# Decay matrices of a two-block transformer step: mask matmuls replaced by a rectified difference and a masked product

## Chip, cores and metric

The kernel runs on one core of one Trainium2 chip. The metric is the device time of one execution in microseconds (us), given as the median of several runs. Engines are named as in the profile: PE is TensorE's matmul, PEld its weight load, DVE is VectorE, ACT is ScalarE, POOL is GpSimd, SP is the engine that issues most DMAs.

## The reference

Two blocks work on x of 256 rows by 1024 columns in float32. The first has two layers of attention with a gated output product. The second has two hybrid layers; each runs attention and a state-space scan side by side, joins them in one output product and adds a gated feed-forward part. The scan works in two chunks of 128 rows, with 16 heads in 2 groups. Cut to what the change touches:

```
def segsum_exp(a):
    cs = jnp.cumsum(a, axis=-1)
    diff = cs[..., :, None] - cs[..., None, :]
    t = a.shape[-1]
    mask = jnp.tril(jnp.ones((t, t), dtype=bool))
    return jnp.exp(jnp.where(mask, diff, -jnp.inf))

a = jnp.transpose((dt * a_neg).reshape(bsz, nc, CHUNK, SSM_GROUPS, e), (0, 1, 3, 4, 2))
cb = jnp.einsum('bclgn,bcsgn->bcgls', cc, bc)
m_mat = cb[:, :, :, None] * segsum_exp(a)
y_diag = jnp.einsum('bcgels,bcsgep->bclgep', m_mat, xg)
```

`dt` is positive and `a_neg` negative, so `cs` never rises, so on the kept side of the triangle diff is at most 0. Every layer also starts with a root-mean-square norm of the rows.

## The kernel before

All large products run in two float32r parts: ACT rounds a weight tile (`hi`, line 1367), DVE subtracts (`lo`, line 1033), and PE multiplies three combinations (line 1178). Weights come in chunks of 1 MB in three rotating slots (`raw`); `hi` and `lo` of a chunk are made in two halves, two chunks ahead of their use. `build_schedule` writes one list of steps by hand. Every engine walks this list in order and carries out its part of each step, so an engine's queue is first in, first out, and the place of a step in the list sets what stands behind it on every engine.

A hybrid layer has eight **decay** steps, four heads each, which are written in four pairs: chunk 0 group 0, chunk 1 group 0, chunk 1 group 1, chunk 0 group 1. In one step

- PE puts the mask into a bank (line 1334: a bf16 matmul of `identb` with the mask spread over four heads) and adds the cumulative sum of each head (line 1340, four bf16 matmuls of 128 columns)
- ACT turns each head's 128 columns into `hyb_E` (line 1592, Exp with the other end's negative sum `hyb_ncs` as bias; the mask of -1e30 becomes 0)
- DVE multiplies by `hyb_cb`, the product B C (line 2015, `hyb_MT`)
- PE later multiplies `hyb_MT` with the values (step diag, line 1349, 8 program matmuls for a pair, 16 in the trace). A pair ends in a **join** on DVE (lines 2023 to 2031), a Square on ACT (line 1392), and for chunk 1 a product with the state (line 1355) before the join.

`hyb_cb` is copied from its bank on ACT in the step bback (line 1571). The four scratch banks of PSUM are handed out in turn, so a step that takes a bank waits until the step four banks earlier has freed it:

```
def bank(self):
    n = len(self.banks)
    b = Bank(n % NSCR, self.banks[n - NSCR] if n >= NSCR else None)
```

By this count the first diag of pair 1 takes the bank of the second decay step of that pair, which ACT frees (`b.freed = (s, "scalar")`), and the second decay step of pair 4 takes the bank that the join of pair 3 frees.

Three more places are touched. At the start of the program the second half of x is turned, rounded (`first_split`) and its weights, chunk 1, are rounded by the step second_weights. Between the blocks (step second_factor) four Squares of 128x512 (`square`) give the mean square for the first hybrid layer. At the end of the first hybrid layer DVE adds the residual (`added`, line 1865) and multiplies by the gain (`gained`, line 1802) before PE turns the result.

Of the kernel before, what the change touches and what calls it, by code (L numbers as in the profile page):

```python
# [66 lines left out]
C_SEL = C_MASK + 2 * QC + P  # L67
C_ALL = C_SEL + 32
M_SCAN, M_SEL = 2 * QC, 2 * QC + P


def constants():
# [26 lines left out]
    c[:, C_MASK + 2 * QC:C_SEL] = np.where(t > u, NEG, 0.0)  # L99
# [257 lines left out]
def norm_goes_on(sc, mid):  # L357


    def second_half():  # L360
        turn_x(sc, 1, 0)
        squares(sc, 0)

    def factors():
        turn_x(sc, 1, 1)
        squares(sc, 1)
        if mid:
            factor(sc, "first")
            normed_residual(sc)
        else:  # L370
            factor(sc, "h")

    def second_factor():
        squares(sc, 0)
        squares(sc, 1)
        factor(sc, "both")

    sc.soon += [second_half, factors] + [second_factor] * mid
# [169 lines left out]
def hybrid(sc, layer, w, last_gain):  # L548
# [27 lines left out]
    def bback():  # L576
        b1, b2 = sc.bank(), sc.bank()
        s = sc.step("bback", banks=(b1, b2), conv=scan["silu", 0])
        b1.freed = b2.freed = (s, "scalar")
# [46 lines left out]
    def do(f, *x):  # L626
        return [lambda: f(*x)]
# [39 lines left out]
    def next_gain():  # L667
# [3 lines left out]
        0: (do(decay, 1, 1, 0) + do(state, 1), do(decay, 1, 1, 1)),  # L671
        1: (do(turn_y, 0, 0) + do(scanned, 1, 1), do(turn_y, 0, 1) + do(decay, 1, 0, 0) + do(decay, 1, 0, 1)),
# [32 lines left out]
    if layer == 0:  # L705
# [7 lines left out]
        turn_x(sc, 0, 1)  # L713
        add(sc, b1, 1, 1)
        for m in range(M):
            times_gain(sc, 1, m)
# [30 lines left out]
def build_schedule(w):  # L747
# [30 lines left out]
def due(s):  # L778

    if s.kind == "second_weights":  # L780
        return [(1, 0), (1, 1)]
# [8 lines left out]
def half_of(c, half):  # L790
# [7 lines left out]
    "taps": ("tensor", "scalar"), "mid_gain": ("vector",), "square": ("scalar",), "meansq": ("vector", "gpsimd"), "newton": ("vector",), "added": ("vector",),  # L798
# [9 lines left out]
    "bback": ("tensor", "scalar"), "xback": ("tensor", "scalar", "gpsimd"), "state": ("tensor", "scalar"),  # L808
# [6 lines left out]
def build(nc, t):  # L815
# [41 lines left out]
    masks = keep("masks", [P, 2 * QC + P + 32], BF16)  # L857
    csum = keep("csum", [P, P], BF16)
    identb = keep("identb", [P, P], BF16)
# [38 lines left out]
    def plan(tag, hybrid_):  # L898
# [36 lines left out]
        if hybrid_:  # L935
# [19 lines left out]
            put("ncs", [P, M, SH])  # L955
            put("dif", [P, SH])
# [167 lines left out]
    def _(pe):  # L1124
# [10 lines left out]
        for s in sc.steps:  # L1135
# [194 lines left out]
            elif s.kind == "decay":  # L1330
# [3 lines left out]
                nc.tensor.matmul(bank[:, :], identb[:, :],  # L1334
                                 spread(masks[:, M_SCAN:M_SCAN + P].unsqueeze(1), [P, 4, P]), start=True, stop=False)
                for i in range(4):
# [3 lines left out]
                    last = nc.tensor.matmul(seg, spread(pick, [96, P]), csum[0:96, :], start=False, stop=i == 3)  # L1340
# [18 lines left out]
    def _(act):  # L1359
# [35 lines left out]
        for s in sc.steps:  # L1395
# [28 lines left out]
            elif s.kind == "square":  # L1424
# [4 lines left out]
                square_sum(h[:, s.m, s.n * 512:(s.n + 1) * 512], sumsq[:, 2 * s.m + s.n:2 * s.m + s.n + 1], s)  # L1429
            elif s.kind == "ev_kv":  # L1430
# [138 lines left out]
            elif s.kind == "bback":  # L1569
                act.wait_ge(sem["bback", "tensor"], s.i + 1)  # L1570
                nc.scalar.activation(Hb["cb"][:, :, :, :].rearrange("p m g l -> p (m g l)"),
                                     psum[4 + s.banks[0].at][:, :], ACT.Copy)
# [12 lines left out]
            elif s.kind == "decay":  # L1585
# [97 lines left out]
    def _(dve):  # L1683
# [46 lines left out]
        def set_up():  # L1730
# [4 lines left out]
            nc.vector.tensor_copy(identb[:, :], ident)  # L1735
# [40 lines left out]
        for s in sc.steps:  # L1776
# [51 lines left out]
            elif s.kind == "meansq":  # L1828
                sq, ms, _, _ = norm_parts(s)
                if s.what == "y":  # L1830
                    dve.wait_ge(sem["join", "scalar"], s.of)
                    done(ts(ms, sq, 1.0 / 512, EPS, ALU.mult, ALU.add), s)
                else:
# [144 lines left out]
            elif s.kind == "sums":  # L1978
                dve.wait_ge(sem["sums", "tensor"], s.i + 1)
                bank = psum[4 + s.bank.at]  # L1980
                chained(ts(Hb["ncs"][:, :, :].rearrange("p m s -> p (m s)"), bank[:, 0:32], -1.0, None, ALU.mult))
                tt(Hb["dif"][:, :], bank[:, 32:48], Hb["ncs"][:, 0, :], ALU.add)
# [97 lines left out]
```

## Time and profile before

| what | value |
|---|---|
| median of 3 runs | 880.14 us (880.09 to 880.61) |
| profiled execution, its own time | 879.62 us |
| its span, first to last instruction | 877.7 us |
| granted TensorE clock, mean | 0.998 |
| busy: PE, DVE, ACT, POOL | 864.6, 567.0, 512.4, 125.5 us |

The span is the time from the first to the last profiled instruction; the execution's own time is 1.9 us more. Busy time of PE is modelled at the ends of its matmuls. A row of the timeline gives start, duration, engine, line, operation, output<-inputs, shape and count, and in brackets how long the engine had been idle and what released it.

### The profile page before, as it was taken

The numbers are of one execution on the slowest core, as the hardware profiler recorded it, in microseconds if no ns is written. First come the engines' busy times: TensorE is split into PE (matmuls) and PEld (weight loads), VectorE is DVE, ScalarE is ACT, GpSimd is POOL, SyncE is SP. The second block draws the span as 40 slices with busy tenths as digits, with TensorE's granted clock in tenths as the row PEclk, the third lists the DMA queues.
The fourth block names the chain that finished last, engine by engine and source line by source line (L and its number), as shares of the span: only waits on it lengthen the run. The fifth ranks groups of instructions, "written<-read, shape, count | busy, mean of one in ns | idle before, by whom it ended". The sixth has DMA issues, their size and how long they took to land. (4 is left out here: it accounts for less than half of the span.)

```text
span 877.7 us, 12103 instructions
## 1 busy us (share of the span) xinstructions
PE 864.6 (99%) x4426; PEld 701.9 (80%) x4426; DVE 567.0 (65%) x1004; ACT 512.4 (58%) x911; POOL 125.5 (14%) x99
## 2 busy tenths in 40 slices
PE   8999999999999999999999999999999999999996
PEld 6877888778877878888888888877878888888885
DVE  6966866767766778755555446566887755555444
ACT  6668466765878865644444334768865644444332
POOL 0122054110153510000000000153410000000000
PEclk9999999999999999999999999999999999999999
DMA  8723563445444345655555555444245665555531
GB/s 308 277 65 119 171 200 134 145 144 173 149 139 144 99 143 186 210 183 187 192 192 190 194 191 171 147 142 144 97 144 168 212 196 192 190 178 178 194 124 48
DMA packets 94749, 146.15 MB, mean 167 GB/s; under 512 B 6500, under 2 KB 54884, under 8 KB 94692
## 3 DMA queue, kind: packets, MB, share of 16 engines
q1 hardware_dynamic: 92804, 139.52, 48.1%
q0 software_dynamic: 1296, 4.72, 1.7%
q10 hardware_dynamic: 592, 1.15, 0.4%
q8 instruction: 36, 0.59, 0.3%
q14 instruction: 21, 0.17, 0.1%
HBM read 144.32 MB, written 1.05 MB: 166 GB/s over the span
## 5 line engine op out<-in xcount | busy, mean ns | idle before, releaser
L1033 DVE TENSOR_TENSOR lo<-raw,hi 128x1024 fp32r<-128x1024 f32 (+1 forms) x244 | 300.5, 1258 | 117.3 <-ACT hi L1367 114.4
L1367 ACT ACTIVATE hi<-raw 128x1024 fp32r<-128x1024 f32 (+1 forms) x260 | 266.7, 1059 | 106.5 <-PE bank L1178 100.9
L1178 PE MATMUL bank<-hi,xT_hi 128*128 128x512 f32 (+2 forms) x736 | 290.4, 395 | 1.2 <-DVE lo L1033 0.5
L1178 PE MATMUL bank<-hi,xT_lo 128*128 128x512 f32 (+2 forms) x736 | 282.6, 384 | 0.0
L1178 PE MATMUL bank<-lo,xT_hi 128*128 128x512 f32 (+2 forms) x736 | 281.8, 383 | 0.0
L1178 PEld LDWEIGHTS bank<-hi,xT_hi 128*128 128x128 f32 x736 | 138.3, 188 | 32.3 <-issue 6.4
L1178 PEld LDWEIGHTS bank<-hi,xT_lo 128*128 128x128 f32 x736 | 138.2, 188 | 28.1
L1178 PEld LDWEIGHTS bank<-lo,xT_hi 128*128 128x128 f32 x736 | 138.5, 188 | 25.1 <-issue 0.5
L1178 PE MATMUL bank<-hi,hT 128*128 128x512 f32 x352 | 109.6, 390 | 0.0
L1178 PEld LDWEIGHTS bank<-hi,hT 128*128 128x128 f32 x352 | 66.1, 188 | 13.7
L1178 PE MATMUL bank<-lo,hT 128*128 128x512 f32 x176 | 68.5, 389 | 0.0
L1178 PE MATMUL bank<-hi,oT_hi 128*128 128x512 f32 x160 | 66.9, 418 | 0.0
L1178 PE MATMUL bank<-hi,oT_lo 128*128 128x512 f32 x160 | 62.6, 391 | 0.0
L1178 PE MATMUL bank<-lo,oT_hi 128*128 128x512 f32 x160 | 62.4, 390 | 0.0
L1466 ACT ACTIVATE silu_gate<-bank,rms 128x256 f32<-128x256 f32 x44 | 20.7, 475 | 53.5 <-PE bank L1178 53.5
L1033 POOL TENSOR_TENSOR lo<-raw,hi 128x1024 fp32r<-128x1024 f32 x16 | 39.0, 2445 | 68.4 <-ACT hi L1367 68.4
L1871 DVE SCALAR_TENSOR_TENSOR quarter<-bank,rms,silu_gate 128x256 f32<-128x256 f32 x44 | 19.3, 479 | 44.2 <-ACT silu_gate L1466 44.2
L2002 DVE SCALAR_TENSOR_TENSOR hyb_acc<-bank,taps,hyb_acc 128x255 f32<-128x255 f32 (+2 forms) x72 | 29.2, 475 | 25.1 <-ACT hyb_acc L1559 25.1
L1633 POOL TENSOR_TENSOR rms<-rms,power 128x2 f32<-128x2 f32 (+1 forms) x9 | 6.1, 675 | 251.3 <-DVE rms L1843 246.7
L1178 PEld LDWEIGHTS bank<-lo,hT 128*128 128x128 f32 x176 | 33.0, 188 | 6.7
L1413 ACT ACTIVATE hT<-bank 128x512 fp32r<-128x512 f32 x22 | 12.1, 596 | 42.1 <-PE bank L1126 42.1
L1178 PEld LDWEIGHTS bank<-hi,oT_hi 128*128 128x128 f32 x160 | 30.1, 188 | 7.1 <-issue 1.8
(247 smaller groups left out, 950.9 us busy)
## 6 DMA issues: line engine op xcount, KB each, us to landing
raw<-in_w_in SPq DMA_DIRECT2D x26, 1024.0 KB, 5.0
raw<-in_w_gate SPq DMA_DIRECT2D x44, 512.0 KB, 3.8
raw<-in_w_up SPq DMA_DIRECT2D x44, 512.0 KB, 4.8
raw<-in_w_down SPq DMA_DIRECT2D x22, 1024.0 KB, 4.8
raw<-in_w_out SPq DMA_DIRECT2D x20, 1024.0 KB, 5.0
raw<-in_w_in_b SPq DMA_DIRECT2D x10, 1024.0 KB, 5.0
raw<-in_w_in_a SPq DMA_DIRECT2D x8, 1024.0 KB, 7.1
raw<-in_w_in_a SPq DMA_DIRECT2D x4, 256.0 KB, 4.9
```

The costliest lines, as they stand in the source:

```text
L1033: return engine.tensor_tensor(lo[r][:, cols], raw[c.i % RAW][:, cols], hi[r][:, cols].bitcast(F32), ALU.subtract)
L1178: last = nc.tensor.matmul(bank[:, 0:wd], still[a], mv[r][:, off:off + wd], start=c.first and i == 0 and j == 0, stop=c.last and i == len(t ...
L1367: nc.scalar.activation(hi[c.i % SPLIT][:, cols], raw[c.i % RAW][:, cols], ACT.Copy)\
L1413: done(nc.scalar.activation(out, bank[:, :], ACT.Copy), s)
L1466: last = nc.scalar.activation(sil[s.i % 2][:, m, :], bank[:, 0:UPW], ACT.Silu, scale=rms[:, 1, m:m + 1])
L1633: nc.gpsimd.tensor_tensor(rs, ms, power[:, 0:1] if s.what == "out" else power[:, :], ALU.pow).then_inc(sem["meansq", "gpsimd"], 1)
L1871: last = stt(quarter[s.buf][:, m * UPW:(m + 1) * UPW], psum[2 * s.block["pair"] + m][:, UPW:2 * UPW], rms[:, 1, m:m + 1], sil[s.i % 2][:, ...
L2002: ins = stt(acc[:, tap:S], x[:, 0:S - tap], cw[:, 3 - tap, ct:ct + 1], acc[:, tap:S], ALU.mult, ALU.add)
```

## The change

It does seven things. The mask matmul of each decay step goes, and each head's matmul starts and stops its own columns. ACT computes Relu(cs - difference), four times 128 columns, then waits for the last of them and applies one Exp with scale -1 over all 512 columns in place; off the kept side of the triangle this gives numbers up to 1 instead of 0. The triangle is put into `hyb_cb` instead: its eviction moves from ACT to DVE and multiplies by `upper`, and the bank is freed by DVE. DVE makes a further copy `hyb_cs` in the step sums. In the output product the decay step 1,1,1 moves ahead of the state product and 1,0,0 moves from after turn_y(0,1) to before it. At the program's start the two halves of chunk 1 are rounded each ahead of one half of x. Between the blocks, two Squares over whole rows replace four over half rows and one DVE addition. At the end of the first hybrid layer the gain of row block 0 comes ahead of the addition of row block 1.

```
     def second_factor():
-        squares(sc, 0)
-        squares(sc, 1)
-        factor(sc, "both")
+        for m in range(M):
+            sc.step("row_square", m=m, added=sc.added[0, m])
+        a = sc.step("meansq", what="both", before=sc.steps[-1])
+        sc.rstd = sc.step("newton", what="both", before=a)
...
-        b1.freed = b2.freed = (s, "scalar")
+        b1.freed, b2.freed = (s, "vector"), (s, "scalar")
         scan["bback"] = s
...
     out_product(sc, w["out"], 12, {
-        0: (do(decay, 1, 1, 0) + do(state, 1), do(decay, 1, 1, 1)),
-        1: (do(turn_y, 0, 0) + do(scanned, 1, 1), do(turn_y, 0, 1) + do(decay, 1, 0, 0) + do(decay, 1, 0, 1)),
+        0: (do(decay, 1, 1, 0) + do(decay, 1, 1, 1) + do(state, 1), ()),
+        1: (do(turn_y, 0, 0) + do(scanned, 1, 1) + do(decay, 1, 0, 0), do(turn_y, 0, 1) + do(decay, 1, 0, 1)),
...
         turn_x(sc, 0, 1)
+        times_gain(sc, 1, 0)
         add(sc, b1, 1, 1)
-        for m in range(M):
-            times_gain(sc, 1, m)
+        times_gain(sc, 1, 1)
...
         first = [first_turn(sc, 1, m) for m in range(M)]
+        sc.step("second_weights")
         first_split(sc, first[0])
         sc.step("second_weights")
         first_split(sc, first[1])
...
     if s.kind == "second_weights":
-        return [(1, 0), (1, 1)]
+        return [(1, s.i)]
...
-                nc.tensor.matmul(bank[:, :], identb[:, :],
-                                 spread(masks[:, M_SCAN:M_SCAN + P].unsqueeze(1), [P, 4, P]), start=True, stop=False)
                 for i in range(4):
...
-                    last = nc.tensor.matmul(seg, spread(pick, [96, P]), csum[0:96, :], start=False, stop=i == 3)
+                    last = nc.tensor.matmul(seg, spread(pick, [96, P]), csum[0:96, :], start=True, stop=True)
...
+            elif s.kind == "row_square":
+                ended(act, s.added, "vector")
+                done(nc.scalar.activation(Hb["xs"][:, s.m, :], h[:, s.m, :], ACT.Square,
+                                          accum_out=sumsq[:, s.m:s.m + 1]), s)
...
-                nc.scalar.activation(Hb["cb"][:, :, :, :].rearrange("p m g l -> p (m g l)"),
-                                     psum[4 + s.banks[0].at][:, :], ACT.Copy)
...
-                                                ACT.Exp, bias=Hb["ncs"][:, m, hh:hh + 1])
-                done(last, s)
+                                                ACT.Relu, scale=-1.0, bias=Hb["cs"][:, m, hh:hh + 1])
+                link(act, "scalar", last)
+                e = Hb[f"E{s.i % 2}"][:, :, :]
+                done(nc.scalar.activation(e, e, ACT.Exp, scale=-1.0), s)
...
+                nc.vector.tensor_copy(Hb["cs"][:, :, :].rearrange("p m s -> p (m s)"), bank[:, 0:32])
...
+            elif s.kind == "bback":
+
+                dve.wait_ge(sem["bback", "tensor"], s.i + 1)
+                done(tt(Hb["cb"][:, :, :, :].rearrange("p m g l -> p (m g) l"),
+                        psum[4 + s.banks[0].at][:, :].rearrange("p (a l) -> p a l", l=P),
+                        spread(upper.unsqueeze(1), [P, 4, P]), ALU.mult), s)
```

ACT at pair 1 of a hybrid layer, before (`hyb_st` is the eviction of the state product; line numbers are those of each version):

```order
L1534 ACTIVATE oT_hi<-hyb_o 128x4x128 x2
L1367 ACTIVATE hi_65<-raw_62 128x1024
L1592 ACT_TABLE_LOAD
L1592 ACTIVATE hyb_E_133<-bank,hyb_ncs 128x128 x4
L1592 ACTIVATE hyb_E_134<-bank,hyb_ncs 128x128 x4
L1583 ACTIVATE hyb_st<-bank 128x512
```

The same place now:

```order
L1537 ACTIVATE oT_hi<-hyb_o 128x4x128 x2
L1366 ACTIVATE hi_65<-raw_62 128x1024
L1593 ACTIVATE hyb_E_132<-bank,hyb_cs 128x128 x4
L1597 ACT_TABLE_LOAD
L1597 ACTIVATE hyb_E_132<-hyb_E_132 128x512
L1593 ACTIVATE hyb_E_133<-bank,hyb_cs 128x128 x4
L1597 ACTIVATE hyb_E_133<-hyb_E_133 128x512
L1584 ACTIVATE hyb_st<-bank 128x512
```

Each group of four is followed by a wide Exp, and the table load stands behind the first group. There are as many table loads as before. ACT from pair 3 to pair 4, in the output product, before:

```order
L1592 ACT_TABLE_LOAD
L1592 ACTIVATE hyb_E_133<-bank,hyb_ncs 128x128 x4
L1583 ACTIVATE hyb_st<-bank 128x512
L1367 ACTIVATE hi_64<-raw_61 128x1024
L1592 ACTIVATE hyb_E_134<-bank,hyb_ncs 128x128 x4
L1367 ACTIVATE hi_65<-raw_62 128x1024
L1416 ACTIVATE oT_hi<-bank 128x4x128
L1392 ACTIVATE junk,rmy<-hyb_xs 128x512
L1367 ACTIVATE hi_65<-raw_62 128x1024
L1416 ACTIVATE oT_hi<-bank 128x4x128
L1592 ACTIVATE hyb_E_133<-bank,hyb_ncs 128x128 x4
L1592 ACTIVATE hyb_E_134<-bank,hyb_ncs 128x128 x4
```

The part of it from the Square of pair 3's join (`junk`) on, now:

```order
L1391 ACTIVATE junk,rmy<-hyb_xs 128x512
L1593 ACTIVATE hyb_E_132<-bank,hyb_cs 128x128 x4
L1597 ACTIVATE hyb_E_132<-hyb_E_132 128x512
L1366 ACTIVATE hi_65<-raw_62 128x1024
L1415 ACTIVATE oT_hi<-bank 128x4x128
L1593 ACTIVATE hyb_E_133<-bank,hyb_cs 128x128 x4
L1597 ACTIVATE hyb_E_133<-hyb_E_133 128x512
L1366 ACTIVATE hi_66<-raw_63 128x1024
```

The first step of pair 4 stands right behind the Square; the second stays behind a `hi` and an `oT_hi` and now also behind the first step's Exp. Both steps of pair 3 stand ahead of `hyb_st`. ACT at the program's start, where `hi_65<-raw_62` is chunk 1 and first_x_59 and first_x_60 are the second half of x, before:

```order
L1377 ACTIVATE hi_64<-raw_61 128x512 x3
L1422 ACTIVATE xT_hi<-first_x_58 128x4x128
L1422 ACTIVATE xT_hi<-first_x_59 128x4x128
L1367 ACTIVATE hi_65<-raw_62 128x1024 x2
L1422 ACTIVATE xT_hi<-first_x_60 128x4x128
```

Now:

```order
L1376 ACTIVATE hi_64<-raw_61 128x512 x3
L1421 ACTIVATE xT_hi<-first_x_58 128x4x128
L1366 ACTIVATE hi_65<-raw_62 128x1024
L1421 ACTIVATE xT_hi<-first_x_59 128x4x128
L1366 ACTIVATE hi_65<-raw_62 128x1024
L1421 ACTIVATE xT_hi<-first_x_60 128x4x128
```

The first half of chunk 1 now stands ahead of the first rounding of the second half of x; DVE's subtractions moved in the same way.

## Rows read from the trace of the kernel before

**Rows 1.** The page, busy time of each engine (us, share, instructions).

```profile
PE 864.6 (99%) x4426; PEld 701.9 (80%) x4426; DVE 567.0 (65%) x1004; ACT 512.4 (58%) x911; POOL 125.5 (14%) x99
```

**Rows 2.** Groups by line and form, PE: busy us, mean ns of one.

```profile
L1340 PE MATMUL bank<-csum,masks 96*128 96x128 bf16 x64 | 6.2, 218 | 0.0
L1334 PE MATMUL bank<-masks,identb 128*128 128x512 bf16 x16 | 6.2, 385 | 0.0
```

**Rows 3.** Chain that ended last, at a decay step: start, us on it.

```profile
624.97 0.23 PE bank L1334
625.20 0.22 PE bank L1340 x4
```

**Rows 4.** Timeline of ACT, DVE and PE at pair 1.

```profile
296.06 1.28 ACT L1592 ACT_TABLE_LOAD   x1
297.36 2.18 ACT L1592 ACTIVATE hyb_E<-bank,hyb_ncs 128x128 f32<-128x128 f32 x8
299.64 0.69 DVE L2015 TENSOR_TENSOR hyb_MT<-hyb_E,hyb_cb 128x512 f32<-128x512 f32 x1 [0.34 <-ACT hyb_E L1592]
299.90 1.90 PE L1349 MATMUL bank<-hyb_xg,hyb_MT 128*128 128x64 f32 x16
```

**Rows 5.** Timeline of ACT, DVE and PE at pair 2.

```profile
303.64 0.63 ACT L1392 ACTIVATE junk<-hyb_xs 128x512 bf16<-128x512 f32 x1 [1.70 <-DVE hyb_xs L2031]
305.22 2.16 ACT L1592 ACTIVATE hyb_E<-bank,hyb_ncs 128x128 f32<-128x128 f32 x8
307.47 1.11 DVE L2015 TENSOR_TENSOR hyb_MT<-hyb_E,hyb_cb 128x512 f32<-128x512 f32 x1 [0.34 <-ACT hyb_E L1592]
308.19 1.89 PE L1349 MATMUL bank<-hyb_xg,hyb_MT 128*128 128x64 f32 x16
```

**Rows 6.** Timeline of ACT, PE and DVE at pair 3 and its join.

```profile
316.92 1.14 ACT L1592 ACTIVATE hyb_E<-bank,hyb_ncs 128x128 f32<-128x128 f32 x4
321.41 2.22 PE L1349 MATMUL bank<-hyb_xg,hyb_MT 128*128 128x64 f32 x16
324.59 0.69 DVE L2023 TENSOR_TENSOR hyb_xs<-bank,hyb_xs 128x512 f32<-128x512 f32 x1 [0.38 <-PE bank L1355]
326.76 0.69 DVE L2031 TENSOR_TENSOR hyb_xs<-hyb_xs,hyb_z 128x512 f32<-128x512 f32 x1
```

**Rows 7.** Timeline of ACT and PE at pair 4.

```profile
327.49 0.63 ACT L1392 ACTIVATE junk<-hyb_xs 128x512 bf16<-128x512 f32 x1 [5.28 <-DVE hyb_xs L2031]
329.55 2.17 ACT L1592 ACTIVATE hyb_E<-bank,hyb_ncs 128x128 f32<-128x128 f32 x8
331.68 2.00 PE L1349 MATMUL bank<-hyb_xg,hyb_MT 128*128 128x64 f32 x16 [0.25 <-DVE hyb_MT L2015]
```

**Rows 8.** DMA issues at 4.0 to 4.8 us: KB, us from issue to landing.

```profile
raw<-in_w_in_a SPq DMA_DIRECT2D x1, 1024.0 KB, 8.6
```

**Rows 9.** Timeline at the start: SP (issues), ACT, DVE and PE.

```profile
4.49 20.95 SPq L1093 DMA_DIRECT2D raw<-in_w_in_a  x6
13.22 1.99 ACT L1367 ACTIVATE hi<-raw 128x1024 fp32r<-128x1024 f32 x2
14.30 2.36 DVE L1033 TENSOR_TENSOR lo<-raw,hi 128x1024 fp32r<-128x1024 f32 x2 [0.26 <-ACT hi L1367]
15.67 0.47 PE L1178 MATMUL bank<-hi,xT_hi 128*128 128x512 f32 x1 [0.55 <-DVE lo L1033]
```

**Rows 10.** Timeline of ACT and PE between the blocks.

```profile
223.42 0.63 ACT L1392 ACTIVATE junk<-h 128x512 bf16<-128x512 f32 x1 [0.47 <-DVE h L2043]
225.06 0.63 ACT L1392 ACTIVATE junk<-h 128x512 bf16<-128x512 f32 x1
228.80 0.47 PE L1178 MATMUL bank<-hi,xT_hi 128*128 128x512 f32 x1 [0.45 <-ACT hyb_q L1447]
```

**Rows 11.** Timeline of DVE and PE at the end of the first hybrid layer.

```profile
542.82 0.68 DVE L1865 TENSOR_TENSOR h<-bank,h 128x512 f32<-128x512 f32 x1
544.15 0.33 PE L1126 MATMUL bank<-cst,quarter 128*128 128x128 f32 x1 [0.20 <-DVE quarter L1802]
```

More of the change, by code:

```diff
@@ L66 @@
 C_MASK = C_KEEP
-C_SEL = C_MASK + 2 * QC + P
+C_SEL = C_MASK + 2 * QC
 C_ALL = C_SEL + 32
-M_SCAN, M_SEL = 2 * QC, 2 * QC + P
+M_SEL = 2 * QC
 def constants():
@@ L98, in constants @@
             c[:, at:at + P] = np.where(x, 0.0, NEG)
-    c[:, C_MASK + 2 * QC:C_SEL] = np.where(t > u, NEG, 0.0)
     for part in range(3):
@@ L797 @@
     "chunk": ("tensor", "scalar", "vector", "gpsimd"), "columns": ("tensor", "vector"), "first_turn": ("tensor", "vector"), "first_split": ("scalar", "vector"), "gained": ("vector",), "turn": ("tensor", "scalar", "vector"),
-    "taps": ("tensor", "scalar"), "mid_gain": ("vector",), "square": ("scalar",), "meansq": ("vector", "gpsimd"), "newton": ("vector",), "added": ("vector",),
+    "taps": ("tensor", "scalar"), "mid_gain": ("vector",), "square": ("scalar",), "row_square": ("scalar",), "meansq": ("vector", "gpsimd"), "newton": ("vector",), "added": ("vector",),
     "ev_kv": ("scalar",), "ev_q": ("scalar",), "ev_z": ("scalar",), "ev_x": ("scalar",),
@@ L807 @@
     "sums": ("tensor", "vector", "scalar"), "conv": ("tensor", "scalar", "vector"), "conv_silu": ("scalar",),
-    "bback": ("tensor", "scalar"), "xback": ("tensor", "scalar", "gpsimd"), "state": ("tensor", "scalar"),
+    "bback": ("tensor", "scalar", "vector"), "xback": ("tensor", "scalar", "gpsimd"), "state": ("tensor", "scalar"),
     "decay": ("tensor", "scalar", "vector"), "diag": ("tensor",), "off": ("tensor",),
@@ L856, in build @@
     cst = keep("cst", [P, C_KEEP])
-    masks = keep("masks", [P, 2 * QC + P + 32], BF16)
+    masks = keep("masks", [P, 2 * QC + 32], BF16)
     csum = keep("csum", [P, P], BF16)
-    identb = keep("identb", [P, P], BF16)
     ones = keep("ones", [P, P])
@@ L955, in plan @@
             put("ncs", [P, M, SH])
+            put("cs", [P, M, SH])
             put("dif", [P, SH])
@@ L1734, in set_up @@
             ts(sinks[:, 1, :], sinks[:, 0, :], -1.0, None, ALU.mult)
-            nc.vector.tensor_copy(identb[:, :], ident)
             chained(nc.vector.tensor_copy(masks[:, :], stage[:, :]))
@@ L1832, in _ @@
                     done(ts(ms, sq, 1.0 / 512, EPS, ALU.mult, ALU.add), s)
+                elif s.what == "both":
+                    ended(dve, s.before, "scalar")
+                    done(ts(ms, sumsq[:, 0:M], 1.0 / D, EPS, ALU.mult, ALU.add), s)
                 else:
@@ L2010, in _ @@
                 m, g = s.mg
-                ended(dve, s.bback, "scalar")
+                ended(dve, s.bback, "vector")
                 dve.wait_ge(sem["decay", "scalar"], s.i + 1)
```

## Prediction, made before the changed kernel ran

> **What bounds the kernel now.** I read the page's busy times first: PE is busy for 864.6 of 877.7 us, DVE for 567.0, ACT for 512.4 [rows 1]. So PE sets the time nearly everywhere, and an edit counts by what it takes off PE's queue and by what it makes PE wait for. ACT and DVE are idle a third of the time, but that is an average. So next I read, pair by pair, when ACT finishes `hyb_E`, when DVE has multiplied it, and when PE needs the product. In pair 1 the last Exp ends at 297.36 + 2.18 = 299.54, DVE's second product runs from 299.64 to 300.33, and PE starts its 16 passes at 299.90; the second eight need that product and start halfway, at about 300.8 [rows 4]. The cover is about 0.5 us. In pair 2 the second product ends at 307.47 + 1.11 = 308.58 and is needed at 308.19 + 0.9 = 309.1 [rows 5]: again 0.5 us. In pairs 3 and 4 there is none: the 16 passes take 2.22 instead of 1.90 [rows 4, 6], and PE waits 0.25 for the first product of pair 4 [rows 7]. So ACT and DVE are idle on average and just in time here. The second hybrid layer repeats the pattern; I work one layer and double it.
>
> **What is removed.** On the chain a mask matmul takes 0.23 and the four sums 0.22 [rows 3]. The 385 ns of the group rows is a modelled length of overlapping matmuls [rows 2], not a cost. Without the mask a step gives back 0.22; 16 steps give 16 x 0.22 = 3.5 us, or 0.44 a pair, if nothing else is late.
>
> The row shows four bf16 sums with four weight loads in 0.22, or 55 ns each [rows 3]. The Trainium skill (TensorE: Matmul & The Clock Gate, LDWEIGHTS) gives a load of 128 columns as columns/1.2 ns, 107 ns; by that, an estimate, four loads take 0.43 and a step without its mask would be no shorter. The row disagrees, although its first load could hide behind the mask; I keep that as a rival below.
>
> **What is added on ACT.** Four Exp of 128 columns are done after 1.14 [rows 6], and eight after 2.18, so a further group adds 1.04 [rows 4]. The trace has no Relu; its neighbour is this Exp: same bank, same width, one bias column. Bounds: a Square moves 512 columns in 0.63 in one instruction [rows 5], so four Relus that move as many can't take less than about 0.63; above, nothing points over 1.14. I take 1.14 and 1.04, since the neighbour has the same width and count, and width is what makes four narrow ones dear. The wide Exp of 512 columns from SBUF is nearest to that Square, 0.63; four narrow ones bound it from above, 1.14 [rows 6]. It waits for the last Relu, so nothing of it overlaps: a step ends 0.63 later than before and the second step of a pair 2 x 0.63 = 1.26 later. The next group may start about 0.1 before the Exp ends, as neighbours do, so I use 1.15 for a pair.
>
> Pair 1. Relu needs no new table, so the first group runs from 296.06 to 297.15 ahead of the load; load 1.28 and Exp 0.63 end at 299.05 [rows 4]. The second group ends at 300.05, its Exp at 300.7, its product at 301.4. The first diag takes the bank that this second step frees, so it can't start before 300.75, while PE without the masks would be there at 299.90 - 0.44 = 299.46. PE waits 1.3; set against before, everything behind is 300.75 - 299.90 = 0.85 late. Its second eight would start at 301.65, after the product.
>
> Pair 2. Its chain starts with PE's diag of pair 1 (join, Square, `hi`, then the steps), so it moves along with the 0.85. Within it, Exp of the second step ends 1.15 later, and the product at 308.58 + 1.15 = 309.75 against a need of 309.1 - 0.44 = 308.65: PE waits 1.1. Against before 0.65 is lost, if DVE's product still takes 1.11; if GpSimd no longer runs beside it and it takes 0.69 [rows 4, 5], 0.25. I take 0.35, so 1.2 since the layer's start.
>
> Pair 3. The second step now stands ahead of `hyb_st`: Relu from 315.6, load, Exp to 318.6, second step to 320.3, its product by about 321.4 (DVE's order has two `lo` ahead). That is in time for the second eight (321.41 - 0.44 + 0.9 = 321.9), so the excess of 0.32 [rows 4, 6] goes. PE would be 0.44 + 0.32 earlier, but the second step of pair 4 needs the bank of the join, which ends at 326.76 + 0.69 = 327.45 [rows 6]. The two `hi` behind `hyb_st` end about 1.4 later, and the `lo` and `oT_lo` ahead of the join with them; DVE is then free at about 324.75, 0.15 later than the join's start [rows 6]. So of 0.76 about 0.6 is kept as PE's lead and 0.2 or so is waited.
>
> Pair 4. Its first step no longer waits behind `hi` and `oT_hi`. Square at 327.65, first group from 328.3 to 329.4, Exp to 330.0. From Square to Exp there were 2.06 us before [rows 7], of which 0.6 was the Square; the remaining 1.45 of `hi` and `oT_hi` run now, to 331.4. Second group 1.14, Exp 0.63, product 0.69: 333.9. PE's second eight started at 331.68 + 0.9 = 332.6 [rows 7] and start now at 334.0. PE waits about 2.4 and everything behind is 1.4 late, counted from pair 3's start. This is the largest term: two steps that were issued back to back after `oT_hi` took 2.17 [rows 7], and now the second begins only there and is serial.
>
> Layer: 1.2 + 1.4 = 2.6 late, with the 8 masks (1.8) already taken off. Two layers: **+5.2**.
>
> **`hyb_cb` and `hyb_cs`.** DVE gains a masked product of 0.7 (as the bank-reading add, 0.69 [rows 6]) and a copy of 0.2 at points where it waits afterwards; ACT loses a copy. PE takes the bank more than 0.5 later. Cost nothing; up to 0.3 a layer if that cover is gone.
>
> **The start.** Chunk 1 is issued at 4.49 and lands 8.6 later, at 13.1 [rows 8, 9]. ACT already starts its `hi` at 13.22 [rows 9], so it can't come forward. What changes is that x's rounding (0.63) now waits behind it, and on DVE x's subtraction (0.69) comes after `lo` instead of before. `lo` still starts at about 14.3 and takes 1.2; x's part ends at 16.1, and PE starts at 16.15 instead of 15.67 [rows 9]. **+0.5**; at best 0, if the landing were earlier in most executions.
>
> **Between the blocks.** The second row's data is ready at 223.42; the last of four Squares starts at 225.06 and ends at 225.7 [rows 10]. Now the second whole-row Square starts at 223.42 and takes 1.05 (a `hi` of 1024 columns is half of 1.99 [rows 9]) and 0.2 for its sum: 1.1 earlier, and DVE saves an add of 0.2. PE's wait of 0.45 [rows 10] goes, and nothing else is that late: **-0.5**.
>
> **End of the first hybrid layer.** The add at 542.82 to 543.5 stands ahead of the gain for which PE waits 0.20 [rows 11]. Moved behind, it frees 0.6: **-0.3** at most with PE's restart; 0.2 by the row.
>
> **Sum.** 5.2 + 0.5 - 0.5 - 0.3 = +4.9 on the profiled 879.62 us (span 877.7 and 1.9 around it): 884.5. The median stands 0.5 above that execution, so the median comes to **885.0 us**.
>
> **Rivals.**
> - ScalarE keeps up, faster. At the lower bound of 0.63 a group, a pair takes 4 x 0.63 = 2.5 against 2.18, an extra of 0.3 that the cover of 0.5 hides. The products would be in time and only the savings were left: -3.5 for masks, -0.6 for the excess and the wait in pairs 3 and 4 (two layers, in part), -0.8 and +0.5 elsewhere: 880.1 - 4.4 = 875.7, say 876. For it: engines are a third idle. Against it: covers of 0.5 against 1.15. It decides where a pair's extra falls under 0.5. Chance 0.18.
> - Half covered, no change: pair 4's lateness is the one that I built from most pieces. Without it a layer loses 1.2 - 0.6 = 0.6, two 1.2, in all 881; with pair 2 free too, 880. Chance 0.12.
> - Later still: GpSimd slows both products of pair 2 (0.4 more a layer), the join of pair 3 slips by 0.3, and PE's waits run on into late `lo`: 2 x 0.7 to 2 x 1.5 more, 886.5 to 888. Chance 0.12.
> - The change doesn't shorten PE: the loads behind the removed masks are no longer hidden and fill the gap. PE waits for the products at every pair anyway, so most of these 3.5 us are spent in waits already and little comes on top: 885 to 888. Chance 0.04.
> - Forecast, 882.5 to 887.5: 0.54.
>
> **Numbers.** Differences under 0.2% (1.8 us) can't be told from no change. Slower: 0.54 + 0.12 + 0.04 = 0.70; same 0.12; faster 0.18. The range leaves out the faster case below 878 (0.15) and anything above 889: 878 to 889.
>
> **What would show it.** No row of line 1334; about 0.22 between groups of sums. PE waits for `hyb_MT` (line 2015 before) of 1 to 2.5 us: first diag of pair 1 about 0.85 late, the longest wait in pair 4's second half. ACT: Relu groups of 1.1, Exp of 0.63, the second pair-4 group starting after `oT_hi`. PE's first matmul of chunk 1 at about 16.1 and not at 15.67. No wait at 228.8 and 544. It is wrong if Relu or the wide Exp is much shorter than its neighbour, or if ACT reaches pair 4 earlier than its queue lets me see.

## Result, and the profile after

The changed kernel takes 888.58 us (median of 4 runs, 885.99 to 890.33) against 880.20 for the kernel before beside it (880.09 to 880.61). The ratio is 1.0094 with a 95% interval of 1.0082 to 1.0106: 8.4 us slower. The forecast was 885.0, in a range of 878 to 889, so direction and range held and the size came out 3.6 us short. But 888.58 lies above the forecast's own band (882.5 to 887.5) and above the times of all four rivals (888 at most); it is inside the range only by the margin that the range adds on top. The spread is news of its own: 4.3 us from run to run where the kernel before spreads over 0.5. The profiled execution is the fastest of the four: 885.99 us, span 884.1, mean granted clock 0.996.

The page of the changed kernel answers to [rows 1]. PE's busy time is 0.9 us less, while the span is 6.4 more. So PE has less to do, as intended, and waits more.

```profile
PE 863.7 (98%) x4410; PEld 701.5 (79%) x4410; DVE 566.7 (64%) x1006; ACT 520.0 (59%) x921; POOL 125.2 (14%) x99
```

Here is what PE waited for in the changed kernel, the rows that are new or grew: engine, tile and line that waited, what it waited for, us in total, times, and the longest.

```profile
PE bank L1348 <- DVE hyb_MT L2021: 5.7, 6, 2.0
PE bank L1348 <- ACT hyb_E L1597: 1.5, 2, 0.8
PE bank L1329 <- POOL hyb_xgd L1680: 0.8, 2, 0.4
PE bank L1339 <- DVE hyb_xs L2043: 0.4, 1, 0.4
```

Before, PE waited 0.5 us in all for `hyb_MT`. Now it waits 5.7 for it, 1.5 for ACT's Exp (which frees the bank of pair 1's diag), 0.8 for GpSimd's `hyb_xgd` and 0.4 for the join's bank.

Pair 1 of the first hybrid layer, on ACT, DVE and PE, answers to [rows 4] (start, duration in us, then idle time before and its releaser in brackets):

```profile
295.86 1.12 ACT L1593 ACTIVATE hyb_E<-bank,hyb_cs 128x128 f32<-128x128 f32 x4
297.00 1.28 ACT L1597 ACT_TABLE_LOAD   x1
298.29 0.63 ACT L1597 ACTIVATE hyb_E<-hyb_E 128x512 f32<-128x512 f32 x1
298.83 1.12 ACT L1593 ACTIVATE hyb_E<-bank,hyb_cs 128x128 f32<-128x128 f32 x4
299.99 0.63 ACT L1597 ACTIVATE hyb_E<-hyb_E 128x512 f32<-128x512 f32 x1
300.72 0.69 DVE L2021 TENSOR_TENSOR hyb_MT<-hyb_E,hyb_cb 128x512 f32<-128x512 f32 x1 [1.00 <-ACT hyb_E L1597]
300.76 1.97 PE L1348 MATMUL bank<-hyb_xg,hyb_MT 128*128 128x64 f32 x16 [0.77 <-ACT hyb_E L1597]
```

Four Relus are done after 1.12, the Exp takes 0.63, and the second group starts only when the first Exp is nearly over. PE's diag starts at 300.76; it waits for the bank. Before, it started at 299.90 [rows 4].

Pair 2, on ACT, DVE, GpSimd and PE, answers to [rows 5]:

```profile
307.45 0.63 ACT L1597 ACTIVATE hyb_E<-hyb_E 128x512 f32<-128x512 f32 x1
309.14 0.63 ACT L1597 ACTIVATE hyb_E<-hyb_E 128x512 f32<-128x512 f32 x1
308.17 1.07 DVE L2021 TENSOR_TENSOR hyb_MT<-hyb_E,hyb_cb 128x512 f32<-128x512 f32 x1 [1.50 <-issue]
309.86 0.83 DVE L2021 TENSOR_TENSOR hyb_MT<-hyb_E,hyb_cb 128x512 f32<-128x512 f32 x1 [0.62 <-ACT hyb_E L1597]
307.65 1.04 POOL L1678 TENSOR_TENSOR hyb_xs<-hyb_xs,small 128x512 f32<-128x512 f32 x1
308.78 1.37 POOL L1680 TENSOR_TENSOR hyb_xgd<-hyb_xg,hyb_dec 128x512 f32<-128x512 f32 x1
309.30 1.10 PE L1348 MATMUL bank<-hyb_xg,hyb_MT 128*128 128x64 f32 x8 [0.51 <-DVE hyb_MT L2021]
310.75 1.10 PE L1348 MATMUL bank<-hyb_xg,hyb_MT 128*128 128x64 f32 x8 [0.34 <-DVE hyb_MT L2021]
```

Read the ends. GpSimd's first instruction ends at 308.69, and DVE's first product at 309.24; GpSimd's second ends at 310.15, and DVE's second product at 310.69. Either product ends 0.55 us behind GpSimd and takes 1.07 and 0.83 instead of 0.69. The kernel before already had this at the same place: the second product of [rows 5] takes 1.11 and ends at 308.58, again 0.55 behind the end (308.03) of GpSimd's instruction:

```profile
306.58 1.45 POOL L1675 TENSOR_TENSOR hyb_xs<-hyb_xs,small 128x512 f32<-128x512 f32 x1
```

Pair 4 answers to [rows 7]:

```profile
332.55 0.58 ACT L1415 ACTIVATE oT_hi<-bank 128x512 fp32r<-128x512 f32 x1
333.02 1.13 ACT L1593 ACTIVATE hyb_E<-bank,hyb_cs 128x128 f32<-128x128 f32 x4
334.19 0.63 ACT L1597 ACTIVATE hyb_E<-hyb_E 128x512 f32<-128x512 f32 x1
334.90 0.69 DVE L2021 TENSOR_TENSOR hyb_MT<-hyb_E,hyb_cb 128x512 f32<-128x512 f32 x1 [0.41 <-issue]
335.65 1.10 PE L1348 MATMUL bank<-hyb_xg,hyb_MT 128*128 128x64 f32 x8 [2.02 <-DVE hyb_MT L2021]
```

The second group starts at 333.02, behind `oT_hi`, its product at 334.90, and PE's second eight at 335.65 after 2.0 us of waiting.

Last, the clock. Windows of the second hybrid layer of the changed kernel: busy time of PE, PEld, DVE, ACT and POOL, then the granted clock (PEclk), DMA share and GB/s. Below it, two of PE's main matmuls there.

```profile
644.00:646.00 2.00, 2.00 (x11) 1.42 (x11) 0.98 (x1) 1.99 (x3) 0.00 (x0) 0.80 0.11 41
646.00:648.00 2.00, 2.00 (x5) 1.33 (x4) 1.38 (x3) 0.45 (x1) 0.00 (x0) 0.50 0.00 0
648.00:650.00 2.00, 2.00 (x9) 1.53 (x7) 1.38 (x2) 0.55 (x2) 0.00 (x0) 0.85 0.00 0
```

And PE's timeline:

```profile
646.74 0.63 PE L1179 MATMUL bank<-lo,oT_hi 128*128 128x512 f32 x1
648.75 0.39 PE L1179 MATMUL bank<-hi,oT_hi 128*128 128x512 f32 x1
```

Pair 2's waits end at 643.90. From about 645 to 648.6 the granted clock is 0.5, the 1.2 GHz level: there the matmuls of 512 columns start 0.43 us apart, against 0.23 behind 648.75. The first hybrid layer has the same waits at pair 2, and both layers have the wait of 2.0 at pair 4, with the clock at 1.00 in this execution.

### The profile page after: what moved, and what is told of

Same layout as the page of the kernel before. It is cut to its first block, busy times and chain, and to the rows that moved or that the text cites. A ratio compares the mean times of both kernels' runs of the same rounds, so it can differ in the third digit from the quotient of the medians.

```text
span 884.1 us, 12079 instructions
## 1 busy us (share of the span) xinstructions
PE 863.7 (98%) x4410; PEld 701.5 (79%) x4410; DVE 566.7 (64%) x1006; ACT 520.0 (59%) x921; POOL 125.2 (14%) x99
## 3 DMA queue, kind: packets, MB, share of 16 engines
q10 hardware_dynamic: 592, 1.08, 0.4%
HBM read 144.26 MB, written 1.05 MB: 164 GB/s over the span
## 4 chain that ended last, share of the span: by engine, by line
PE 81%; ACT 9%; DVE 5%; issue 4%; DMA 1%; SPq 0%; POOLq 0%; POOL 0%; DVEq 0%; ACTq 0%
PE bank L1179 71%; PE bank L1127 5%; ACT hi L1366 2%; ACT hyb_E L1593 2%; PE bank L1348 1%; DVE hyb_acc L2008 1%; DMA raw<-in_w_in_a 1%; PE bank L1234 1%; PE bank L1231 1%; PE bank L1276 1%; DVE lo L1034 1%; ACT hyb_E L1597 1%; ACT attn_prob L1512 1%; DVE hyb_xs L2043 1%; ACT hyb_acc L1562 0%
```

## Experiments

In all of them the kernel before ran beside the others on the same chip: 880.41, 880.26 and 880.21 us in the three groups. "Shift" below means how much later the same main matmul of PE starts in one trace than in that of the kernel before. It is a reading of one execution each; the medians are of 4 to 11 runs.

**scan_only, rest_only: which half of the change.** The first has only the scan's edits, the second only start, row squares and gain order:

```
 scan_only:  changed kernel, with second_factor, second_weights, due and times_gain as before
 rest_only:  kernel before, with these four as in the changed kernel
```

> Only the edits of the scan (no mask matmuls, Relu and wide Exp, masked product, moved decay steps); start, squares between the blocks and order of the gain as in the kernel before. Theory A (serial Relu and Exp late for PE, and a lower clock after PE's waits on top): the four pairs cost 3.2 us in the first hybrid layer by the changed kernel's trace and 1.9 in the second without its stretch at 1.2 GHz, so 880.2 + 5.1 = 885.3 where the clock holds, and 1.5 to 2.5 more for each stretch at the lower clock: median 886 to 889, spread over some us. Rival B (most of the loss lies in the start and the other edits): under 883.5.

> Only the start order, the row squares and the order of gain and addition; decay matrices as before. Read from the shift of the same matmuls between the two traces: start +0.6 (of which a part may be the arrival of x in that one execution), between the blocks -0.7, end of the first hybrid layer -0.4: 879.7, from 879.2 to 880.2, clock 0.998 as before and a spread under 0.6. Rival B: 883 or more.

scan_only took 890.84 us (888.65 to 892.69; ratio 1.0117, 1.0100 to 1.0134), rest_only 878.99 (878.74 to 879.38; 0.9984, 0.9976 to 0.9993). The two differences, +10.4 and -1.4, sum to 9.0, near the whole change's 8.4. So the scan is the loss, and the rest is a gain. Both came out beyond what I expected: scan_only above its 886 to 889, rest_only below its 879.2 to 880.2. The windows of scan_only show why its median is so high: the granted clock falls at three places, after pair 4 of both layers and at pair 2 of the second.

```profile
334.00:344.00 10.00, 7.98 (x36) 6.52 (x35) 7.42 (x15) 6.14 (x12) 0.69 (x1) 0.83 0.33 105
644.00:654.00 10.00, 9.14 (x40) 6.58 (x39) 5.88 (x8) 6.96 (x15) 2.90 (x3) 0.83 0.31 105
670.00:684.00 14.00, 12.03 (x51) 10.06 (x50) 9.77 (x16) 6.71 (x14) 1.32 (x2) 0.76 0.37 107
```

**start_only, squares_only, gain_only: the small terms one by one.**

```
 start_only:    +        sc.step("second_weights")        (ahead of first_split(sc, first[0]))
                +        return [(1, s.i)]
 squares_only:  -        squares(sc, 0) ...               +  two steps row_square
 gain_only:     +        times_gain(sc, 1, 0)             (ahead of add(sc, b1, 1, 1))
```

> The kernel before with only the new order at the start (each half of chunk 1 rounded ahead of one half of x). Forecast step: +0.5, 880.9. Rival: the order costs nothing or gains, since the kernel with all three small edits came out at 878.99 and their shifts between the blocks and at the end of the first hybrid layer sum to 1.1 of 1.4 us: 880.1, from 879.8 to 880.4. The start varies by up to 2 us from run to run with the arrival of x, in both kernels.

> The kernel before with only the two row squares between the blocks. Forecast step -0.5; the shift between the traces of before and changed there is -0.7: 879.6 against 880.3, range 879.4 to 879.9. Rival (the wait is only moved to the next one): 880.3.

> The kernel before with only the gain of row block 0 ahead of the addition of row block 1 at the end of the first hybrid layer. Forecast step -0.3; the shift in the traces is -0.4: 879.9 against 880.3, range 879.8 to 880.1. Rival (no change): 880.3.

Measured: start_only 880.32 (880.00 to 880.76; ratio 0.9999, 0.9990 to 1.0008), squares_only 879.45 (879.14 to 879.74; 0.9992, 0.9983 to 1.0001), gain_only 879.67 (879.25 to 880.82; 0.9997, 0.9988 to 1.0006). As differences of medians: +0.1, -0.8 and -0.5, in sum -1.2 (gain_only just below its 879.8 to 880.1), against -1.4 for the three together. Each alone is within the interval of no change; the sum is not. Why the start costs nothing is seen when PE's first matmul of chunk 1 in the changed kernel is set beside the timeline of ACT and PE in gain_only, which has the start of the kernel before. First the changed kernel:

```profile
16.27 0.50 PE L1179 MATMUL bank<-hi,xT_hi 128*128 128x512 f32 x1 [0.48 <-DVE xT_lo L1820]
```

and gain_only:

```profile
13.42 0.63 ACT L1422 ACTIVATE xT_hi<-first_x 128x512 fp32r<-128x512 f32 x1 [2.86 <-DVE first_x L1810]
13.96 1.99 ACT L1367 ACTIVATE hi<-raw 128x1024 fp32r<-128x1024 f32 x2
16.41 0.47 PE L1178 MATMUL bank<-hi,xT_hi 128*128 128x512 f32 x1 [0.55 <-DVE lo L1033]
```

In the profiled execution of the kernel before PE started chunk 1 at 15.67 [rows 9], but it was an execution in which x had arrived early: in gain_only x comes 0.7 later, ACT rounds x from 13.42, `hi` of chunk 1 stands behind it until 13.96, and PE starts at 16.41. In the new order `hi` does not stand behind x. So in these two traces the orders end within 0.15 us of each other. In start_only's own trace chunk 1 landed 0.6 later (its `hi` from 13.91) and PE started at 16.89, so single executions don't decide this term; the medians do.

**plain_exp, plain_old: the change without Relu and wide Exp.**

```
-                                                ACT.Relu, scale=-1.0, bias=Hb["cs"][:, m, hh:hh + 1])
-                link(act, "scalar", last)
-                e = Hb[f"E{s.i % 2}"][:, :, :]
-                done(nc.scalar.activation(e, e, ACT.Exp, scale=-1.0), s)
+                                                ACT.Exp, scale=1e-3, bias=Hb["dt"][:, m, hh:hh + 1])
+                done(last, s)
 plain_old: the same, and the two lines of out_product as before
```

> The changed kernel with one Exp per head straight from the bank in place of Relu and wide Exp, with a small scale and hyb_dt as the bias so that nothing overflows: it leaves out the true decay factors. Theory A: the products are in time again; 880.2 - 3.5 for the masks + 1.1 for two waits for hyb_xgd - 0.5 for the other edits = 877.3, range 876 to 879, clock 0.998, spread under 1. Rival C (the new order, the masked product on DVE or the loads behind the missing mask matmuls cost what was lost): 884 or more.

> The changed kernel with one Exp per head from the bank (small scale and hyb_dt as bias: it leaves out the true decay factors) and with the decay steps in their old places: what is left of the change without Relu and wide Exp. In the trace of the same kernel in the new order PE waits 1.26 us in pair 4 for a second product that starts behind oT_hi and oT_lo. Theory A2 (with short groups the new place of pair 4 costs, with long ones it does not matter): 0.3 to 0.5 a layer better than 877.78 and fewer stretches at the lower clock, 876.3 to 877.5, spread under 1. Rival: the order is indifferent here too, 877.8.

plain_exp took 877.78 (877.37 to 881.26; ratio 0.9980, 0.9970 to 0.9990). Seven of its eleven runs lie from 877.37 to 877.80, the other four from 879.66 to 881.26, with clocks of 0.994 to 0.996. The median is where theory A put it, the spread of 3.9 is not: I had expected under 1. plain_old took 878.29 (877.95 to 878.60; 0.9978, 0.9969 to 0.9987). So the masks are worth 1.3 us over rest_only (878.99 to 877.7, the median of the seven), not 3.5. What took the rest is seen in PE's rows of plain_exp:

```profile
295.67 0.70 PE L1329 MATMUL bank<-hyb_xgd,hyb_bt 128*128 128x512 f32 x1 [0.39 <-POOL hyb_xgd L1678]
332.25 1.10 PE L1348 MATMUL bank<-hyb_xg,hyb_MT 128*128 128x64 f32 x8 [1.10 <-DVE hyb_MT L2018]
```

PE waits 0.39 for `hyb_xgd` ahead of the state product, since without the two mask matmuls of pair 1 it arrives before GpSimd is done (start to start 0.55 is lost, where 0.12 was lost before), and 1.10 for the second product of pair 4, which stands on DVE behind `oT_lo`. My expectation that the old order would be better here was wrong: it is 0.6 worse than those seven, which the intervals of the two ratios can't tell apart but the traces show too (PE's start to start shows 0.69 lost in pair 3 and 0.85 in pair 4 in place of 1.26 in pair 4), but it has no run with the clock down.

**one_relu: the length of a group.**

```
+                last = nc.scalar.activation(Hb[f"E{s.i % 2}"][:, :, :].rearrange("p i l -> p (i l)"),
+                                            psum[4 + s.bank.at][:, :], ACT.Relu, scale=-1.0,
+                                            bias=Hb["cs"][:, m, hh:hh + 1])
```

> The changed kernel with one Relu of 512 columns for the four heads of a step, with the first head's column as bias (it leaves out the other heads' own sums). A group falls from 1.12 to 0.63 if the cost is the number of instructions, and a pair's ACT work from 3.3 to 2.35 against 2.18 before. The prediction's first rival put the point of decision at an extra of 0.5 a pair: then most waits go and 876 to 879 is left. Theory A2, with two waits for hyb_xgd and pair 4 in its new place: 878 to 880. Rival (the wide Exp and its wait are the cost, not the narrow Relus): 884 or more.

Measured 881.64 (880.36 to 883.43; ratio 1.0015, 1.0006 to 1.0024), between the two expectations. A group takes 0.67. Pair 1's wait is gone. Pair 2's waits are what they were (0.53 and 0.34). ACT, DVE, GpSimd and PE at pair 2 of one_relu:

```profile
307.41 0.63 ACT L1597 ACTIVATE hyb_E<-hyb_E 128x512 f32<-128x512 f32 x1
306.89 2.97 DVE L2021 TENSOR_TENSOR hyb_MT<-hyb_E,hyb_cb 128x512 f32<-128x512 f32 x2 [1.05 <-issue]
307.94 1.37 POOL L1680 TENSOR_TENSOR hyb_xgd<-hyb_xg,hyb_dec 128x512 f32<-128x512 f32 x1
308.46 1.10 PE L1348 MATMUL bank<-hyb_xg,hyb_MT 128*128 128x64 f32 x8 [0.53 <-DVE hyb_MT L2021]
309.91 1.10 PE L1348 MATMUL bank<-hyb_xg,hyb_MT 128*128 128x64 f32 x8 [0.34 <-DVE hyb_MT L2021]
```

The second Exp ends at 308.04, and PE gets its product 1.9 later, at 309.91. DVE's two products take 2.97 in place of 1.4 and end at 308.41 and 309.86, each 0.55 behind a GpSimd instruction (307.86 and 309.31). DVE and GpSimd at the same place in plain_exp, whose pair 2 has no wait at all:

```profile
306.79 0.69 DVE L2018 TENSOR_TENSOR hyb_MT<-hyb_E,hyb_cb 128x512 f32<-128x512 f32 x1 [0.84 <-issue]
306.94 1.45 POOL L1676 TENSOR_TENSOR hyb_xs<-hyb_xs,small 128x512 f32<-128x512 f32 x1
```

Here DVE's first product starts 0.15 ahead of GpSimd's instruction, takes its usual 0.69, and it is GpSimd that takes 1.45 in place of 1.04. In one_relu GpSimd had started at 306.82, 0.07 ahead of DVE. So at pair 2 the order in which the two engines start decides, and the one that comes second pays. The Trainium skill (GPSIMD Engine Reference, Specifications) says that GpSimd's SBUF interfaces are shared with VectorE, with contention for DVE instructions that have two SBUF inputs; `hyb_MT` has two, and the traces agree. Over all kept traces, the two kernels' and the runs', 40 products of pair 2 began while a GpSimd instruction had more than 0.1 us to go, and all 40 end 0.55 us after it; plain_exp's second is one of them (308.93 behind 308.39). Sixteen others began in the last 0.03 to 0.07 us of a GpSimd instruction and took their usual time, 0.67 to 0.69.

**old_order, both_early: the place of the decay steps.**

```
 old_order:   the two lines of out_product as before
 both_early:  1: (do(turn_y, 0, 0) + do(scanned, 1, 1) + do(decay, 1, 0, 0) + do(decay, 1, 0, 1), do(turn_y, 0, 1)),
```

> The changed kernel with the decay steps of the output product back in their old places (1,1,1 after the state product; 1,0,0 after turn_y). Forecast step: the new place puts pair 4's second step behind hi and oT_hi and so costs; the old place would be better. Theory A2, from the trace of the changed kernel: both steps then start behind oT_hi, at 331.4 in its times, and end 3.3 later at 334.7, against 334.8 measured, so the second product is as late as now, and the first 1 us late on top without moving the second: median 887.5 to 890. Rival E (the new place is what costs): 885 or less.

> The changed kernel with both decay steps of pair 4 ahead of hi and oT_hi. Theory A: Square ends at 329.9, second Exp at 333.2, second product at 334.0 against a need of 333.4 to 333.9: the wait of 2.2 in pair 4 shrinks to 0.6 or less in both layers, hi and oT_hi come 1.7 later and hide it, and fewer stretches at the lower clock follow: 888.6 - 3.2 - 1 = 884.5, range 883 to 886. Rival F (oT_hi or hi 1.7 later becomes the next wait): 887 or more.

old_order took 888.59 (886.92 to 889.12; ratio 1.0090, 1.0077 to 1.0104), the same as the changed kernel: with long groups the second product of pair 4 is as late from either place. both_early took 886.78 (886.54 to 887.92; 1.0075, 1.0061 to 1.0089), 1.8 better instead of 4. PE's waits in it:

```profile
PE bank L1348 <- DVE hyb_MT L2021: 2.5, 6, 0.5
PE bank L1179 <- DVE oT_lo L1829: 1.8, 2, 0.9
PE bank L1339 <- DVE oT_lo L1829: 1.6, 2, 0.8
```

Pair 4's wait of 2.0 fell to 0.35. But `oT_lo` of turn_y(0,1) comes 1.4 later and the main matmuls wait 0.9 for it, and the second step's sums, which now stand earlier, wait 0.8 for a bank that `oT_lo` of turn_y(0,0) frees. The rival of that expectation was half right. That fewer stretches at the lower clock would follow was wrong: the five clocks are 0.994 to 0.996, and in the profiled execution the clock fell behind pair 4 in either layer (0.72 granted from 335 to 341 us, 0.76 from 669 to 676), although PE's longest wait in the scan is 0.92.

**dve_diff: the difference on DVE.**

```
+                for i in range(4):
+                    last = ts(Hb[f"E{s.i % 2}"][:, i, :], psum[4 + s.bank.at][:, i * P:(i + 1) * P],
+                              Hb["ncs"][:, m, hh:hh + 1], 0.0, ALU.add, ALU.min)
...
+            for x in (scan["decay", g, m, 0], s):
+                scan["weigh", g, m, x.q] = sc.step("weigh", q=x.q, mg=(m, g), decay=x)
```

> The changed kernel with the rectified difference on DVE, four tensor_scalar of 128 columns from the bank (add hyb_ncs, minimum with 0), for both steps of a pair ahead of either masked product, and only the wide Exp left on ACT; the bank is freed after the differences. Theory A (the serial work on ACT is the cost): 4 x 0.2 to 0.25 on DVE twice, then Exp 0.63 and product 0.69: a pair's last product ends about 3.1 us after the first sums can be read, against 4.0 now and 2.9 before; waits of 0.2 to 0.6 a pair stay: 880.5 to 884, spread under 2.5. Rival G (DVE gets late with lo, and PE waits there): 886 or more.

Measured 896.25 (894.44 to 897.32; ratio 1.0178, 1.0164 to 1.0192), the worst of all. The estimate for pair 1 was right (PE loses 0.36 there, not 1.0), and eight differences take 2.15 us. But in pair 4, where the two steps stand apart, I had put both products behind the second step's differences:

```profile
297.15 2.15 DVE L2017 TENSOR_SCALAR hyb_E<-bank,hyb_ncs 128x128 f32<-128x128 f32 x8
332.32 1.12 DVE L2017 TENSOR_SCALAR hyb_E<-bank,hyb_ncs 128x128 f32<-128x128 f32 x4
336.83 1.12 DVE L2017 TENSOR_SCALAR hyb_E<-bank,hyb_ncs 128x128 f32<-128x128 f32 x4
337.86 0.68 DVE L2026 TENSOR_TENSOR hyb_MT<-hyb_E,hyb_cb 128x512 f32<-128x512 f32 x1
```

The first differences are ready at 333.44, their product starts at 337.86, and PE waits up to 2.9 us for it. Pair 3, whose steps stand together, is late too:

```profile
322.38 2.15 DVE L2017 TENSOR_SCALAR hyb_E<-bank,hyb_ncs 128x128 f32<-128x128 f32 x8
325.19 2.00 PE L1351 MATMUL bank<-hyb_xg,hyb_MT 128*128 128x64 f32 x16 [1.25 <-DVE hyb_MT L2026]
```

Its sums are done by 317.1, but on DVE the differences stand behind two `lo` until 322.38, and PE waits 1.25, which is near to rival G. By PE's shift, pair 3 costs 2.1 us more than in the changed kernel and pair 4 2.3 more. So the place that I gave to the products is only a part of the failure, and the idea with another order on DVE is open.

**fill: the clock.**

```
+                if s.q == 1 and s.i % 8 in (3, 7):
+                    for _ in range(3 if s.i % 8 == 3 else 16):
+                        nc.tensor.matmul(psum[4 + s.bank.at][:, 256:512], csum[0:96, :],
+                                         spread(csum[0:96, :].unsqueeze(1), [96, 2, P]), start=True, stop=True)
```

> The changed kernel with bf16 matmuls of 256 columns put where PE waits for the second product: 3 in pair 2, 16 in pair 4, into columns of the bank that diag writes afterwards. Theory A on the clock (it falls after PE's waits in the scan): most stretches at 1.2 GHz go, median 884 to 886.5, spread under 2.5, granted clock 0.996 or more. Rival D (the clock falls whatever PE does there): median 888 to 889 and clocks from 0.990 to 0.996 as in the changed kernel.

Measured 885.61 (885.07 to 885.73; ratio 1.0057, 1.0043 to 1.0071): 3.0 below the changed kernel, with 0.7 of spread in place of 4.3 and clocks of 0.997 to 0.999. PE's timeline at pair 4 of fill:

```profile
333.65 1.91 PE L1344 MATMUL bank<-csum 96*128 96x256 bf16 x16
335.83 1.10 PE L1352 MATMUL bank<-hyb_xg,hyb_MT 128*128 128x64 f32 x8 [0.27 <-DVE hyb_MT L2025]
```

and its windows around pair 4 of either layer:

```profile
334.00:342.00 8.00, 7.73 (x46) 6.43 (x44) 5.63 (x13) 4.53 (x8) 0.69 (x1) 1.00 0.41 131
664.00:674.00 10.00, 9.73 (x58) 7.91 (x57) 6.26 (x11) 7.32 (x15) 0.69 (x1) 1.00 0.34 107
```

The product comes no sooner (335.83 against 335.65), but PE works through most of the wait and the granted clock stays at 1.00. So 3 us of the 8.4 are the clock, and its fall hangs on PE idling at these places. What one stretch at 1.2 GHz costs can be read in old_order, behind pair 4 of the first layer: over its matmuls the shift grows from 3.37 to 4.94, by 1.6 us. By that the 3 us are about two such stretches, an estimate. The Trainium skill (TensorE: Matmul & The Clock Gate, A second HAM failure mode: psum-queue depth-cycling) tells of a kernel in which short idle times of PE between groups of matmuls made the clock fall and rise again. The traces agree: waits of 0.3 to 2 us, then in some executions 3 to 7 us at 1.2 GHz. Not tried was a wait of this size put into the kernel before.

## Why the prediction was right in direction and short in size

The stage sums below are shifts of fill against before, since its clock holds; the changed kernel's own shifts in the first layer agree within 0.1.

- **Pair 1.** Predicted: diag not before 300.75, 0.85 late. Measured 300.76, a shift of +1.0. The sizes behind it held too: groups of 1.12 for 1.14 and 1.04, Exp 0.63. The neighbour rows of Exp and Square [rows 5, 6] gave the price of two instructions that the trace didn't have. The wait for `hyb_xgd` was missed, but in the changed kernel the bank wait behind it swallows it.
- **Pair 2.** Predicted +0.35 net, 0.65 at the upper end, and 0.4 more in a rival. Measured +0.85 net. This is the term of the sum that was mis-sized. The second product was to end at 310.16 if it took 0.69 (308.58 - 0.42 + 1.15 + 0.85); it ends at 310.69. Of these 0.53, 0.23 is that the chain starts 1.08 late at the Square and not 0.85, 0.16 is that the two groups and Exps take 3.47 and not 2.16 + 1.15, and only 0.14 is the product itself, 0.83 instead of 0.69 beside GpSimd. GpSimd has a part in the first piece too: the last DVE product of pair 1's join ends 0.55 behind GpSimd's `hyb_xg` (304.69 behind 304.14), which starts when ACT has evicted the values, and that eviction is 1.08 late behind the longer pair 1 on ACT. So here the length of the chain on ACT and GpSimd both hold pair 2. With groups of 0.67 (one_relu) GpSimd alone still keeps both waits; in plain_exp, which also has no wide Exp and whose first product gets ahead of GpSimd by 0.15, they are gone. The rival "Later still" named GpSimd's hold on both products, and its 0.4 a layer is near the size, but that hold is the smaller part of it.
- **Pairs 3 and 4.** Predicted -0.6 and then +2.0, together +1.4. Measured -0.65 and +1.96, together +1.3. The wait for the join's bank (0.4, forecast about 0.2) and the longest wait in pair 4's second half (2.0, forecast about 2.4) are where they were forecast. That the second step starts "only there" because of its place was right, but old_order shows that the old place ends at the same time.
- **A layer** costs 3.15 and 3.1 instead of 2.6: 6.25 for both, not 5.2.
- **Start.** Predicted +0.5, measured +0.1. The term was worked out from an execution whose x came earlier than in every other profile (by 0.7 us in gain_only).
- **Between the blocks** -0.8 for -0.5, **end of the first hybrid layer** -0.5 for -0.3. Both waits are gone, and both terms were sized low: they went by the waits of 0.45 and 0.20, where PE's start to start loses 0.61 and 0.36 in the trace of the kernel before.
- **The sum** without the clock is 6.25 + 0.1 - 0.8 - 0.5 = +5.05; fill measures +5.2 and the forecast said +4.9. That the forecast stands so near to it is luck: the errors, 1.05 in the scan and -0.9 in the rest, cancelled.
- **The clock** is the term that was not there: +3.0 in the median and nearly all of the spread. The forecast counted waits only by their length. In the kernel before, the clock of the profile's windows is 1.00 all through the scan, with waits of at most 0.3 us for the scan's products, so nothing in it priced a longer one. This term alone puts the result above the forecast's band.
- **The rivals.** "ScalarE keeps up" at 876 was wrong also by its own rule: one_relu has nearly its group (0.67) and an extra of 0.4 a pair and still comes to 881.6, because GpSimd holds pair 2 and pair 4's second step stands behind `oT_hi`, and part of it is the clock (0.994 to 0.998). Its saving of 3.5 for the masks is only 1.3 by plain_exp. That the loads behind the removed masks fill the gap is refuted: at pair 2 from the first sum to the next main matmul there are 0.43 us in the changed kernel (305.39 to 305.82), where with the two masks there were 0.87 (304.46 to 305.33). Each mask does give back its 0.22; the waits take it.

The fastest kernel measured that leaves nothing out is rest_only, 878.99 us: the three small edits without the scan's. It beats both the kernel before and the changed one.

## What to carry to other kernels

A matmul removed from the bounding engine pays only until the engine meets the next thing that it has to wait for: here eight masks of 0.22 a layer ran into GpSimd's product and DVE's queue, and 1.3 of 3.5 us was left even where nothing was added for them. When a change makes PE wait in several places close together, ask for the clock too: here it put 3 us and a spread of 4.3 on top of the waits' own length, and cheap matmuls in the waits showed how much of the loss it was. An instruction that takes longer than its neighbours in the trace before (1.11 for 0.69 in [rows 5]) is worth a look at what ran beside it: that price was readable there. And look at the first microseconds of more than one execution before pricing an edit there.

## What was unexpected of the hardware

- DVE's products with two SBUF inputs that began while a GpSimd instruction had more than 0.1 us to go ended 0.55 us behind it, in 40 of 40 cases; one that began 0.15 us ahead of the next GpSimd instruction took its usual 0.69, and GpSimd 0.4 more.
- Waits of PE of 0.3 to 2 us were followed in some executions by about 3 to 7 us at a granted clock of 0.5, and not in others of the same kernel; with bf16 matmuls in the longer waits the mean clock was 0.997 to 0.999 in all five runs.
- Four TENSOR_SCALAR of 128 columns from PSUM take 1.12 us on DVE, as long as four Relus on ACT (1.12); one Relu of 512 columns takes 0.67.
